# Staging the first token tiles and the second rotary table ahead, interleaving the gate projection with the first query blocks, and keeping one input tile buffer

## The reference, cut to what matters

```python
shift, scale, gate = adaln(c, w_mod[i], b_mod[i])          # silu(c) @ w_mod + b_mod, in three parts
c_shift, c_scale, c_gate = adaln(c_ctx, w_mod[i], b_mod[i])
h_ctx = modulate(rms_norm(ctx, norm_pre_g[i]), c_shift, c_scale)
k_ctx, v_ctx = ...                                          # h_ctx @ columns of w_in
h = modulate(rms_norm(x, norm_pre_g[i]), shift, scale)      # x (16, 4096, 1024)
...
# mixer_sublayer
xa, ga, q, k, v, gb, gm = split_columns(h @ w_in)           # w_in (1024, 5632)
y_a = pool_mixer(xa, pool_w, pool_scale) * silu(ga)
y_b = attend(q, k, v) * silu(gb)      # rotary q, k; keys of +-128 tokens and the 256 of the context
g = sigmoid(gm)
out = (g[..., :D] * (y_a @ w_branch_a) + g[..., D:] * (y_b @ w_branch_b)) @ w_out
...
x_new = x + gate[:, None, :] * rms_norm(out, norm_post_g[i])
```

## Time and profile before

| what | value |
|---|---|
| median of 3 runs | 2321.43 us |
| lowest of them | 2314.51 us |
| the profiled execution | 2318.52 us |
| its span (slowest core, core 0) | 2317.0 us |
| spans of the 8 cores | 2307.3 to 2317.0 us |
| PE busy in the span | 2250.5 us, 97% |
| DVE, ACT, POOL busy | 60%, 51%, 41% |

### The profile page before, as it was taken

One profiled execution on the slowest core, in us unless ns is written; L12 is line 12 of the kernel. 1 busy time (PEld: TensorE's weight loads), 2 busy tenths in 40 slices (PEclk: granted clock), 3 DMA queues, 4 the chain that ended last, 5 costly groups with the idle time before them and its releaser, 6 DMA issues.

```text
span 2317.0 us, 85914 instructions; the slowest of 8 cores (2307.3 to 2317.0 us)
## 1 busy us (share of the span) xinstructions
PE 2250.5 (97%) x33950; PEld 1782.5 (77%) x34016; DVE 1399.0 (60%) x3636; ACT 1191.9 (51%) x2439; POOL 941.2 (41%) x1130
## 2 busy tenths in 40 slices
PE   6779999999999999999999999999999999999998
PEld 1367787787788778778778778778877877887786
DVE  0346666656656665666665665666666566566664
ACT  1145455555555555555545555555555555555453
POOL 1123443443444344344344344444434434443443
PEclk8889999999999999999999999999999999999999
DMA  9972222222222222222322222222222232222211
GB/s 279 185 148 59 70 62 77 61 68 73 62 73 65 76 63 62 77 70 66 87 65 70 77 62 75 66 68 70 62 69 69 63 78 59 75 66 69 60 50 56
DMA packets 173999, 180.30 MB, mean 78 GB/s; under 512 B 136340, under 2 KB 144660, under 8 KB 170280
## 3 DMA queue, kind: packets, MB, share of 16 engines
q1 hardware_dynamic: 171448, 157.96, 24.6%
q0 software_dynamic: 2160, 16.84, 4.3%
HBM read 125.54 MB, written 33.56 MB: 69 GB/s over the span
## 4 chain that ended last, share of the span: by engine, by line
PE 91%; DMA 5%; DVE 1%; issue 1%; POOL 1%; ACT 0%; SPq 0%; POOLq 0%; DVEq 0%; ACTq 0%
PE pb L541 41%; PE pb L534 11%; PE pb L799 10%; PE pb L783 10%; PE pb L694 7%; PE pb L720 6%; PE pb L773 5%; DMA s_ropet<-rope 1%; DMA s_xt<-x 1%; DMA s_scr<-g_rows 1%; DMA s_xt<-ctx 1%; PE pb L347 0%; DMA gg_scr<-s_scr 0%; DVE s_yb L499 0%; DVE s_scr L606 0%
## 5 line engine op out<-in xcount | busy, mean ns | idle before, releaser
L541 PEld LDWEIGHTS pb<-s_hT,s_W 128*128 128x128 bf16 x17408 | 987.1, 98 | 112.6 <-issue 111.0
L541 PE MATMUL pb<-s_hT,s_W 128*128 128x128 bf16 x17408 | 1060.9, 219 | 1.9 <-DVE s_Gb L629 1.9
L697 ACT ACTIVATE s_PT<-pb 128x512 bf16<-128x512 f32 x1264 | 653.1, 610 | 246.2 <-PE pb L694 246.2
L606 DVE TENSOR_TENSOR s_scr<-pb,s_ropet 128x512 f32<-128x512 f32 x256 | 165.0, 686 | 320.4 <-PE pb L541 316.6
L611 POOL TENSOR_TENSOR s_qT<-s_scr 128x512 bf16<-128x512 f32 x128 | 161.6, 1284 | 435.7 <-DVE s_scr L606 435.7
L707 DVE TENSOR_TENSOR s_PT<-s_PT,s_maskb 128x1024 bf16<-128x1024 bf16 x248 | 317.7, 1321 | 0.0
L534 PE MATMUL pb<-s_W,s_hT 128*128 128x512 bf16 (+1 forms) x1472 | 284.9, 343 | 3.4
L783 PE MATMUL pb<-s_ybT,s_wmf 128*128 128x128 bf16 x4096 | 249.6, 219 | 1.1 <-DVE s_scr L764 1.1
L810 POOL TENSOR_TENSOR s_small<-s_small,s_mh 128x1 f32<-128x1 f32 x64 | 35.1, 549 | 527.8 <-DVE s_small L808 527.8
L787 POOL TENSOR_TENSOR s_mgT<-s_ub,s_scr 128x512 bf16<-128x512 f32 x128 | 163.1, 1274 | 181.5 <-DVE s_small L729 173.5
L783 PEld LDWEIGHTS pb<-s_ybT,s_wmf 128*128 128x128 bf16 x4096 | 234.0, 98 | 1.8 <-issue 1.8
(11 more groups left out here) (93 smaller groups left out, 2401.6 us busy)
## 6 DMA issues: line engine op xcount, KB each, us to landing
s_xt<-x SPq DMA_DIRECT2D x64, 512.0 KB, 3.9
s_xr<-x SPq DMA_DIRECT2D x64, 512.0 KB, 3.5
y<-s_xr SPq DMA_DIRECT2D x64, 512.0 KB, 2.6
s_W<-w_in POOLq DMA_DIRECT2D x10, 1024.0 KB, 51.3
s_wmf<-w_mod SPq DMA_DIRECT2D x8, 1024.0 KB, 15.4
s_ropet<-rope SPq DMA_DIRECT2D x64, 128.0 KB, 2.0
s_W<-w_mod SPq DMA_DIRECT2D x4, 1024.0 KB, 20.3
s_xt<-ctx SPq DMA_DIRECT2D x4, 512.0 KB, 9.6
```

The costliest lines, as they stand in the source:

```text
L541: E("pe", lambda e, c=c, k=k: e.matmul(out=pb[:, c * 128:(c + 1) * 128], lhsT=W[:, wblk, k, c * 128:(c + 1) * 128], rhs=h[:, k, :], start= ...
L606: E("dve", lambda e: e.tensor_tensor(out=view(s, 0, [[128, 4], [1, 128]]), in0=view(pbx, 0, [[128, 4], [1, 128]]), in1=view(rp, cs * 128, ...
L697: E("act", lambda e, g=g: e.activation(out=PT[:, jb, g, :], in_=banks[g][0][:, :], func=AF.Exp, scale=0.125), reads=[banks[g][1]], writes= ...
```

## The change

- Input tiles 1, 2 and 3 (context tile 1 and token tiles 0 and 1) are loaded into the fifths 2, 3 and 4 of `PT`, unused until the first scores (`x_place`). Everything else goes through one buffer `xt`; `xt1` is gone. Context tile 1, token tiles 0 and 1 and the table of tile 1 are asked for at the start; token tile 2 when `norm_front` has used context tile 0.
- The rotary table of tile 1 is loaded into `sB`, a tile of the pooling sums that is idle until period 0 (`rope_place`); that of tile 2 is asked for at the end of the new `first_period`, which takes the place of `start_gate` and period -1.
- `first_period` emits `P_kv(0)`, the gate block 4, `P_q(0)`, the gate block 5, then `fold_pool`, `P_xa(0)` and `gb`. `load_w(2)` and `load_w(3)` go ahead of the raw block 1.
- In period 0 the first scores come behind `P_kv(1)`.
- `LAG = 1` keeps the distances of before, with lists of one tile for `ya` and `ybT`. The reciprocals in `small` are written over the denominators.

```diff
-        xs_ = [sb(f"xt{i}", [128, D], F32) for i in range(2)]
+        xt = sb("xt", [128, D], F32)
...
         def first_weights():
             load_w(0, reads=wm_place(3)[1])
+            for blk in (2, 3):
+                load_w(blk)
             E("pool", lambda e: e.dma_start(out=view(PT, 0, [[1, 4096]]), in_=win_d[1]),
...
-        def start_gate():
-            for blk in range(4, 6):
+        def gate_rows(blk):
...
+            if blk == 4:
+                load_cast(flat2(wmf[0]), wb_d, "wmf0", also=wm_place(0)[1])
+                for w in range(9, 11):
+                    load_w(w)
+            else:
+                load_cast(flat2(wmf[1]), wout_d, "wmf1", also=wm_place(1)[1])
...
+        STAGE = {1: 2, 2: 3, 3: 4}
+
+        def x_place(n):
+            if n in STAGE:
+                a = PT[:].bitcast(F32)
+                j = STAGE[n]
+                return (AP(a.tensor, a.offset + j * 1024, [list(a.ap[0]), [1, 1024]]), [bf(f"PT{j}_{g}") for g in range(4)], f"d_x{n}")
+            return xt[:], [bf("xt")], "d_x0"
...
+        def rope_place(t):
+            return (sB, [bf("sB")]) if t == 1 else (ropet, [bf("ropet")])
...
-            vis()
+            if p > 0:
+                vis()
             if p == 0:
                 norm_front()
                 next_load()
             if hasP:
                 P_kv(p + 1)
+            if p == 0:
+                vis()
...
-            if p + 2 < TT:
+            if 0 < p < TT - 2:
                 load_rope(p + 2)
...
-        start_loads()
+        def first_period():
+            P_kv(0)
+            gate_rows(4)
+            q = P_q(0)
+            next(q)
+            next(q)
+            gate_rows(5)
+            fold_pool()
+            P_xa(0)
+            gb(0, 0)
+            mod_pe(turn_pe(), hT[1], "hT1", 0)
+            gb(0, 1)
+            load_rope(2)
+
+        for n in range(2):
+            next_load()
         load_rope(0)
         load_wmod(2)
         load_wmod(3)
-        norm_next()
+        for n in range(2):
+            next_load()
+        load_rope(1)
         mod_block(0)
         load_wmod(4)
+        norm_front()
+        next_load()
         mod_block(1)
         load_wmod(5)
...
-        norm_next()
-        fold_pool()
-        start_gate()
-        for p in range(-1, TT + 1):
+        norm_front()
+        first_period()
+        for p in range(0, TT + LAG):
             period(p)
```

More of the change, by code:

```diff
@@ L248, in build_program @@
         PT = sb("PT", [128, 5, 4, 512], BF16)
-        ya = sb("ya", [128, 512], BF16)
-        Wp = AP(ya[:].tensor, ya[:].offset, [list(ya[:].ap[0]), [128, 4], [1, 128]])
+        ya = [sb(f"ya{i}", [128, 512], BF16) for i in range(LAG)]
+        Wp = AP(ya[0][:].tensor, ya[0][:].offset, [list(ya[0][:].ap[0]), [128, 4], [1, 128]])
         yb = sb("yb", [128, D], BF16)
         hTc = AP(yb[:].tensor, yb[:].offset, [list(yb[:].ap[0]), [128, 8], [1, 128]])
-        ybT = sb("ybT", [128, 8, 128], BF16)
+        ybT = [sb(f"ybT{i}", [128, 8, 128], BF16) for i in range(LAG)]
         mgT = sb("mgT", [128, 8, 128], BF16)
-        small = sb("small", [128, 48], F32)
+        small = sb("small", [128, 24], F32)
         NPB, NTB = 8, 0
@@ new lines, in gate_rows @@
+        def gate_rows(blk):
+            c0 = (blk - 4) * 512
+            t = [next_scr() for _ in range(3)]
+            for j in range(2):
+                E("sp", lambda e, j=j, t=t, c0=c0: e.dma_start(out=t[j][0][0:4, :], in_=grow_d[j:j + 1, c0:c0 + 512].partition_broadcast(4)),
+                  writes=[t[j][1]], dma_sem=dsem(f"d_grow{j}"))
+            pg, pgb = mod_rows(blk)
+            r, rb = t[2]
+            E("dve", lambda e, pg=pg, r=r, t=t: e.tensor_tensor(out=r[0:4, :], in0=pg[0:4, :], in1=t[0][0][0:4, :], op=ALU.add),
+              reads=[pgb, t[0][1]], writes=[rb])
+            E("dve", lambda e, r=r, t=t: e.scalar_tensor_tensor(out=r[0:4, :], in0=r[0:4, :], scalar=32.0, in1=t[1][0][0:4, :],
+                                                           op0=ALU.mult, op1=ALU.mult),
+              reads=[rb, t[1][1]], writes=[rb])
+            E("sp", lambda e, r=r, c0=c0: e.dma_start(out=ggs_d[:, c0:c0 + 512], in_=r[0:BPC, :]), reads=[rb], writes=[bf(f"ggs{blk - 4}")],
+              dma_sem=dsem(f"d_ggs{blk - 4}"))
+            if blk == 4:
[4 more added lines that the diff above has]
+                load_cast(flat2(wmf[1]), wout_d, "wmf1", also=wm_place(1)[1])
@@ L484, in norm_front @@
               reads=[bf("ssb"), bf("mh")], writes=[bf("rstd")])
-            E("act", lambda e: e.activation(out=xsb[:], in_=xt[:], func=AF.Copy, scale=small[:, 2:3]),
-              reads=[xb, bf("rstd")], writes=[bf("xsb")])
+            E("act", lambda e: e.activation(out=xsb[:], in_=xin, func=AF.Copy, scale=small[:, 2:3]),
+              reads=xb + [bf("rstd")], writes=[bf("xsb")])
         def yb_bufs(k):
@@ L601, in P_q @@
             q = qT[t % 2]
-            rp, rpb = ropet, bf("ropet")
+            rp, (rpb,) = rope_place(t)
             def mul(pbx, pbxb, cs):
@@ L666, in pool_gate @@
                   reads=[bf(f"sF{g}"), bf(f"xa{t % 3}")], writes=[bf(f"sF{g}")])
-            E("dve", lambda e: e.tensor_tensor(out=ya[:], in0=view(sF, 0, [[1, 512]]), in1=Ga[:], op=ALU.mult),
-              reads=[bf(f"sF{g}") for g in range(4)] + [bf("Ga")], writes=[bf("ya")])
+            E("dve", lambda e: e.tensor_tensor(out=ya[t % LAG][:], in0=view(sF, 0, [[1, 512]]), in1=Ga[:], op=ALU.mult),
+              reads=[bf(f"sF{g}") for g in range(4)] + [bf("Ga")], writes=[bf(f"ya{t % LAG}")])
         def blocks_of(t):
@@ L748, in ybT_pe @@
                   reads=yb_bufs(c) + [bf("ident")], writes=[tpb], inc=(c == 7))
-            E("dve", lambda e: e.tensor_copy(out=view(ybT, 0, [[1, 1024]]), in_=tp), reads=[tpb], writes=[bf("ybT")])
+            E("dve", lambda e: e.tensor_copy(out=view(ybT[t % LAG], 0, [[1, 1024]]), in_=tp), reads=[tpb], writes=[bf(f"ybT{t % LAG}")])
         def do_ybT(t):
-            transpose_dma(ybT[:], yb[:], [x for k in range(8) for x in yb_bufs(k)], [bf("ybT")])
+            transpose_dma(ybT[t % LAG][:], yb[:], [x for k in range(8) for x in yb_bufs(k)], [bf(f"ybT{t % LAG}")])
         tm_n = [0]
@@ L943, in period @@
             if hasG:
-                late.append((p - 1, out_mm(p - 1)))
+                late.append((p - LAG, out_mm(p - LAG)))
                 flush_out()
```

98 lines of the change are left out of this document (39 added, 59 removed).

## The result

The changed kernel took 2303.22 us (median of 4 runs, 2303.07 to 2303.96) against 2321.43 for the kernel before. The ratio is 0.9928, 95% interval 0.9902 to 0.9955: faster by 0.45 to 1%, well inside 2% but clear of no change. The profiled execution took 2303.15 us; the spans of the cores are 2297.6 to 2301.6 (before 2307.3 to 2317.0). The slowest core is now core 6. All rows of after are from it.

What follows compares the result with a forecast made beforehand. Only the front could gain, where PE waits on the order of work while the DMA engines are full. Terms +7.5 - 18.5 - 2.1 = -13.1 us took the profiled 2318.52 to 2305 us, range 2295 to 2318.

Steps and rivals of the forecast that it cites:

- first period: Start of the kernel up to period 0: the gate's small transfers in series behind gate block 5 cost +7.5 us.
- period 0: After the first period: waits for tile 1's keys and tile 0's queries go, and half a slow-clock stretch: -18.5 us.
- period 1: Period after period 0: the wait for the rotary table of tile 2 goes, -2.1 us.
- The waits: PE's front waits: 11.2 us for tile 1's keys, 5.5 for tile 0's queries, 2.1 for tile 2's table.
- The head: Kernel start: PE's 7.01 us wait at line 359, behind the first norm on DVE, shrinks by 2.4 us.
- the arithmetic of the queue: Queue q1 at the front: transfers land in issue order, and gate block 5 is complete at 86.2 us.
- The first pair of `g_rows` is behind block 5 in q1: 87.2: Gate at the front: this fetch lands at 87.2 us, after gate block 5, with 1 us for itself.
- The floor: End of the front: `w_o` lands at about 160 again, so at most 22.9 us can be gained.
- rival A: Gate's small transfers take little or don't wait behind block 5; bytes decide: -22.9 us, 2295.6 us; chance 0.18.
- One input buffer: Later input loads: the single buffer costs nothing, with 1.2 us to spare; up to 2 us if late twice.
- B: Front's queue q1 gets less than computed: gain gone at 1.33 times the chain, 2337 us at 1.79; chance 0.12.
- C: Period 0 is paced by exponentials and DVE, so half its 18.5 us stays: 2314.7 us; chance 0.15.

Runs made afterwards that it cites:

- e2: Changed kernel without the staging of tile 1's rotary table, which goes into the one table tile `ropet`: 2306.95 us, 0.9913 of the kernel before.
- e3: Kernel before with only the rotary tables' staging added (tile 1's in `sB`, tile 2's asked for a period sooner): 2311.20 us, 0.9934 of the kernel before.
- e10: Changed kernel with the first period's interleaving undone (`fold_pool` and both gate blocks first), tiles and tables still staged: 2306.99 us, 0.993 of the kernel before.
- e11: Changed kernel with the input tiles' staging undone (two buffers in turn), table and interleaving kept: 2318.20 us, 0.9975 of the kernel before.
- e1: Changed kernel with the second pair of `g_rows` fetched right behind the first, into idle tiles: 2306.22 us, 0.9912 of the kernel before.
- e8: Changed kernel with early `g_rows`, and with `gg` and the first residual tile asked for some 30 us later: 2303.49 us, 0.9902 of the kernel before.
- e9: Kernel with early `g_rows` and late residual, weight blocks 9 and 10 not loaded (7 and 8 reused, another result): 2297.57 us, 0.989 of the kernel before.
- e5: Changed kernel with two input buffers from token tile 2 on, each load a tile further ahead: 2307.89 us, 0.992 of the kernel before.
- the sets: Three sets of ten other kernels, each beside the kernel before; the changed kernel ran again in the second (2307.24 us) and third (2306.29 us).

## Why the prediction was right, and where it erred

The time was right: 2305 forecast, 2303.22 measured, with -13.1 us forecast and -15.4 from profile to profile. The place was right. The new longest wait stands in `fold_pool`, behind the gate's second fetch, as forecast, but it is for the gate's bank and not for a cast, and its size (11 us) was too large by 4. Part of the match is luck: the first period erred by 4.9 us one way, the other two terms by 2.6 the other way. Term by term, core 6 after against core 0 before, the slowest of each:

| term | forecast | measured |
|---|---|---|
| first period | +7.5 | 108.08 - 105.5 = +2.6 |
| period 0 | -18.5 | (132.14 - 108.08) - 41.0 = -16.9 |
| period 1 | -2.1 | (167.98 - 132.14) - (183.42 - 146.51) = -1.1 |
| sum | -13.1 | -15.4 |

- **The waits** were read with a gap: after the 11.2 us the next is not the 5.5 for queries but 6.59 us at line 347, for a cast of `fold_pool`. It lies in the 105.5 us of the first period, which the sum takes whole, so the sum stands.
- **The head** was right: PE waits 5.29 us there and not 7.01, and that matmul runs at 22.92, 3.0 us sooner; 2.4 was taken.
- **The first period was over-charged by 4.9 us.** Block 5 landed at 83.3 where the arithmetic of the queue gave 86.2. The step that failed is "The first pair of `g_rows` is behind block 5 in q1: 87.2": it was in use at 80.68 and 82.89, before the whole block was in. DVE's operations ended at 83.6 and not 88.7, 5.1 us early, which is the whole error. Store and fetch (5.9 us, and 8.0 up to the second operation, as the forecast counts it) were taken well, at 6.3 and 7.45. The Trainium skill's fixed 2.0 us a transfer ("DMA: Bandwidth & Descriptors", section "Anatomy of one DMA — SWDGE (gpsimd) path") is given there for transfers that GpSimd issues. These are SyncE's, and the trace disagrees with it for them at the front (5.9 and 8.0 us); the table's median of 2.1 us over the program is near it.
- **Period 0** was right in size and wrong in its reason. "The table of tile 1 is in `sB` long before" is true, but the table isn't what made the 11.2 us go: without its staging (e2) the time is the same, and with it alone (e3) it is 14.8 us below the kernel before. In e2 the table is asked for 14 us sooner, some 11.5 of it by the gate's earlier end (e10's row) and the rest by the queries' place between the gate blocks; in e3 its own tile brings it early. Each removes that wait, so their gains don't add. What I priced at zero on the gain's side, the staging of the tiles, can't be left out: without it SP's queue is blocked by a load that waits for a norm (e11, +11.9).
- **Period 1** gave 1.1 of 2.1 us: the two `gb` blocks after a 1.8 us wait for `yb` take 5.01 us and not 3.61 as in the period before (128.60), at a granted clock of 0.72.
- **The floor** was right as a limit: `w_o` landed at 162.7 (160.5 forecast) and was used 5.3 us later. It binds sooner than I took it, through `w_b` and blocks 9 and 10 (e1, e8, e9). That is why rival A can't be had by mending the chain alone.
- **One input buffer** costs nothing (e5). On ACT the context tile's norm waits for a transpose, as before, and not for its load:

```profile
1017.67 1.06 ACT L495 ACTIVATE s_xsb<-s_xt 128x1024 bf16<-128x1024 f32 x1 [0.71 <-DMA s_hT<-s_xsb]
```

- **Rivals.** B needed a chain 1.33 times as long, and it ended 5 us sooner than forecast (98.2 and not 103.2). C would have left half of period 0's 18.5 us; 1.6 us stayed.

Three things stay open. Why the changed kernel takes 2303 us in the result and 2306 to 2307 in the sets isn't shown; the part after the first output matmul is equal within about 1 us in all versions, so it is in the front, and the slowest core waits for weights in the sets and not in the result's profile. What the tiles' staging is worth alone wasn't run. Whether `g_rows` ahead of block 4 would help wasn't tried.

## What to carry to other kernels

Where a queue issues in order, look for the entry that waits (a load that needs a buffer back) and for the small fetch behind it: giving that load an idle tile was the part of this change that couldn't be left out, while the table's staging, worth 14.8 us in the old kernel, was worth nothing beside the others. Before pricing the removal of a wait, find when the next input lands: here up to 8 us of chain were removed and nothing was gained, since the weights came no sooner. Credit a wait to an edit only after asking which other edit of the same change would remove it too.

## What the runs showed of the hardware

- A 128 KB table landed in 12.1 us at the front and in 2.1 us (median) over the program; 4 KB stored took 5.9 us and 8 KB fetched 6.9 there. The bytes don't explain these times. What differs is the load of the engines: a share of 1.01 at the front and 0.27 in the middle.
- A small transfer can land before a large one that was issued ahead of it in the same queue: `g_rows`, asked for at 56.71, was in use at 80.68, while the half block asked for at about 34 was whole at 83.3.
- A short wait can cost more than its length. After waits of 3.53, 1.31 and 2.34 us (e1) the granted clock fell from 1.00 to between 0.50 and 0.53, and 32 matmuls took 3.5 us and not 1.95; three waits of 7.2 us in all brought about 4.7 us more. It isn't sure: after 1.34 us on one core of the changed kernel (third set), and after 2.70 us on core 2 in the result's profile, 32 of them took 1.95.
- The 8 cores of one chip differ by 9.6 us in the time of the first output matmul before the change, and by 3.5, 5.7 and 3.5 in three profiles after it, with the same program.
